# Second MoE layer: each expert's token rows formed by one-hot products on TensorE, in place of an indirect gather

## The reference, cut to what matters

```python
def _hier_moe(h, w_group, b_group, w_router, b_router, w_gate, w_up, w_down):
    ...
    p_in, e_in = lax.top_k(jax.nn.softmax(lg, axis=-1), TOP_K_IN_GROUP)
    ...
    xb = h_pad[tok_buf].reshape(n_blocks, MOE_BLOCK, d)

    def expert_block(args):
        xe, e = args
        return (jax.nn.silu(xe @ w_gate[e]) * (xe @ w_up[e])) @ w_down[e]

    y = lax.map(expert_block, (xb, blk_e)).reshape(cap, d)
    out = jax.ops.segment_sum(y.astype(jnp.float32) * w_buf[:, None], tok_buf, num_segments=t + 1)
```

## Time and profile before

| | us |
|---|---|
| median of 3 runs | 2418.37 (2416.91 to 2419.72) |
| profiled execution, own time | 2418.02 |
| its span | 2416.1 |
| PE busy, share of the span | 88% |
| DVE, ACT, POOL busy | 45%, 28%, 11% |
| mean DMA rate over the span | 273 GB/s |
| granted TensorE clock, mean over the span | 0.941 of full |

### The profile page before, as it was taken

The page is one execution under the profiler, slowest core; times in us unless marked ns, Lnnn a source line. Parts: engine busy times, 40 slices in busy tenths (PEclk is TensorE's granted clock), DMA queues, the critical chain, the costliest instruction groups (busy, mean ns, idle before and its releaser), DMA issues.

```text
span 2416.1 us, 29462 instructions
## 1 busy us (share of the span) xinstructions
PE 2128.9 (88%) x11370; PEld 1350.4 (56%) x11370; DVE 1089.0 (45%) x1709; ACT 676.7 (28%) x1071; POOL 256.0 (11%) x388
## 2 busy tenths in 40 slices
PE   7899999998899999989797878888789698888887
PEld 5777788886778888856532323333466333333332
DVE  6677754556676455586511111111686322211223
ACT  4243444343334433274211101110446100000000
POOL 2000000010000001000111111111120111111110
PEclk9989999999999999999698989999789699999998
DMA  9745566563656657402899999999911899999996
GB/s 312 261 162 197 196 222 201 202 247 124 239 175 226 209 182 255 107 1 76 309 368 401 414 408 410 403 410 374 296 24 55 346 381 412 423 413 415 416 409 244
DMA packets 178448, 659.87 MB, mean 273 GB/s; under 512 B 18375, under 2 KB 64023, under 8 KB 153136
## 3 DMA queue, kind: packets, MB, share of 16 engines
q1 hardware_dynamic: 159648, 622.65, 67.7%
q0 software_dynamic: 16592, 32.10, 4.2%
q10 hardware_dynamic: 2112, 3.77, 0.4%
HBM read 658.36 MB, written 24.84 MB: 283 GB/s over the span
## 4 chain that ended last, share of the span: by engine, by line
PE 53%; DMA 26%; DVE 12%; ACT 4%; issue 2%; SPq 1%; POOL 1%; ACTq 0%; POOLq 0%; DVEq 0%
PE bank L745 29%; DMA sb_ring<-in_w_up 23%; PE bank L1336 13%; DVE sb_ring_rounded L1978 2%; PE bank L759 2%; PE bank L1360 1%; PE bank L781 1%; ACT sb_hb L1572 1%; DVE sb_st L2182 1%; PE bank L1347 1%; DMA sb_ring<-in_ev_w_in 1%; PE bank L927 1%; PE bank L941 1%; DVE sb_ring_rounded L1985 1%; ACT sb_ring L1432 1%
## 5 line engine op out<-in xcount | busy, mean ns | idle before, releaser
L1336 PE MATMUL bank<-sb_ring,sb_arena 128*64 128x512 f32 x1984 | 508.3, 659 | 134.1 <-DMA sb_ring<-in_w_up 131.3
L745 PE MATMUL bank<-sb_ring_rounded,sb_hT_rounded 128*128 128x512 f32 x2432 | 605.4, 397 | 16.7 <-DVE sb_hT_rounded L1965 5.6
L745 PEld LDWEIGHTS bank<-sb_ring_rounded,sb_hT_rounded 128*128 128x128 f32 x2432 | 459.1, 191 | 116.7 <-issue 10.4
L1336 PEld LDWEIGHTS bank<-sb_ring,sb_arena 128*64 128x64 f32 x1984 | 155.8, 150 | 431.9 <-issue 424.4
L1978 DVE TENSOR_TENSOR sb_ring_rounded<-sb_ring,sb_ring_rounded 128x2048 fp32r<-128x2048 f32 (+1 forms) x142 | 314.9, 2258 | 109.6 <-ACT sb_ring_rounded L1467 105.0
L745 PE MATMUL bank<-sb_ring_rounded,sb_arena_rounded 128*128 128x512 f32 x1408 | 357.0, 395 | 7.7 <-DVE sb_arena_rounded L1965 7.2
L1467 ACT ACTIVATE sb_ring_rounded<-sb_ring 128x2048 fp32r<-128x2048 f32 x146 | 268.0, 1887 | 123.5 <-PE bank L745 98.9
L745 PEld LDWEIGHTS bank<-sb_ring_rounded,sb_arena_rounded 128*128 128x128 f32 x1408 | 266.1, 190 | 63.6 <-DVE sb_arena_rounded L1965 7.4
L1865 ACT ACTIVATE sb_hb<-bank 64x512 f32<-64x512 f32 x64 | 37.8, 590 | 758.6 <-PE bank L1336 758.6
L1360 PE MATMUL bank<-sb_ring,sb_arena 128*64 128x512 f32 x1008 | 230.1, 598 | 3.5 <-DVE sb_arena L2789 3.5
L2789 DVE COPY sb_arena<-bank 128x256 f32<-128x256 f32 x64 | 27.1, 424 | 374.2 <-PE bank L1347 374.2
(11 more groups left out here) (357 smaller groups left out, 1996.3 us busy)
## 6 DMA issues: line engine op xcount, KB each, us to landing
sb_ring<-in_w_down SPq DMA_DIRECT2D x63, 2048.0 KB, 23.1
sb_ring<-in_w_up SPq DMA_DIRECT2D x62, 2048.0 KB, 21.9
sb_ring<-in_w_gate SPq DMA_DIRECT2D x62, 2048.0 KB, 17.7
sb_ring<-in_w_ada SPq DMA_DIRECT2D x48, 1024.0 KB, 7.5
sb_ring<-in_ffn_w_gu SPq DMA_DIRECT2D x44, 1024.0 KB, 7.7
sb_ring<-in_xa_w_kv SPq DMA_DIRECT2D x16, 1024.0 KB, 7.3
sb_ring<-in_ffn_w_down SPq DMA_DIRECT2D x16, 1024.0 KB, 6.6
sb_ring<-in_od_w_in SPq DMA_DIRECT2D x12, 1024.0 KB, 7.5
```

Of the source, the lines that this page charges most:

```text
L745: ins = pe.matmul(bank[b][0:rows, :], rnd(x), rnd(w[:, k, :]), start=start and k == k0 and q == 0, stop=stop and k == k1 - 1 and q == len( ...
L1336: ins = pe.matmul(bank[2 * j + part][part * ROWS:(part + 1) * ROWS, :], mxT[:, j, k, :], w[:, k, :], start=k == 0, stop=k == KD - 1)
```

## The change

In layer 1 the rows of an expert no longer come from DRAM. VectorE turns each token's two pairs into a place number (`places`: 64 times its expert, plus its rank, plus 64 x 31 for every whole block of 64 that lies before it, minus a constant; four columns for two tiles and two picks), and `mark(j, e)` compares it with 64 constants: a 128 x 64 table per token tile that has a one where token p sits in row r of expert e. After every expert 64 is subtracted from all places. `place_rows` multiplies: for each of the 8 pieces of 128 features the two token tiles of `hr` are the stationary operand and the table is the moving one, and the sum of the two is the expert's rows, already turned. That is 16 products in place of 8 transposes. The table for e+2 is made in expert e's step on DVE; the products for e+1 stand where `turn_rows` stood. The first expert's table and products move ahead of the wait for `steps_ready`. Layer 1's store of the tokens to DRAM, the zeroing of `mx`, the gathers, and SP's wait for `rows0` go. `mact`, `mactT` and `mcol` get another home in layer 1, since the arena part that holds `hr` must stay. Layer 0 stays as it was.

```diff
             def experts(l):
                 m = moe[l]
-                pe.wait_ge(*c.next(s["steps_ready"]))
-                less_2 = steps_less_2(pe)
-                steps = less_2 + 2
-                for b in range(8):
-                    claim(b)
+                mact, mactT = act_home[l]
                 def turn_rows(j, e, landed_rows):
+                    if l == 1:
+                        place_rows(j, e)
+                        return
                     ...
+                def place_rows(j, e):
+                    pe.wait_ge(m["marked"], e + 1)
+                    pe.sem_inc(s["passed"], 1)
+                    for k in range(KD):
+                        for t in range(2):
+                            ins = pe.matmul(bank[T0 + j][:, k * ROWS:(k + 1) * ROWS], hr[:, t, k:D:KD], place_marks[:, j, t, :], start=t == 0, stop=t == 1)
+                    ins.then_inc(m["pe_xT"], 1)
+                if l == 1:
+                    claim(T0)
+                    place_rows(0, 0)
+                pe.wait_ge(*c.next(s["steps_ready"]))
...
@@ scalar
-                act.dma_start(DR["tok"][t * P:(t + 1) * P, :], hr[:, t, :]).then_inc(s[f"tok_stored{t % 2}"], 16)
+                if l == 0:
+                    act.dma_start(DR["tok"][t * P:(t + 1) * P, :], hr[:, t, :]).then_inc(s[f"tok_stored{t % 2}"], 16)
...
@@ vector
+            def mark(j, e):
+                m = moe[1]
+                if not (isinstance(e, int) and e == 0):
+                    dve.wait_ge(m["marked"], e)
+                    dve.tensor_scalar(places, places, -float(ROWS), None, ALU.add).then_inc(m["places"], 1)
+                    dve.wait_ge(m["places"], e)
+                since(dve, m["pe_xT"], e - 1)
+                row = cst[:, C_ROW:C_ROW + ROWS].unsqueeze(1).to_broadcast([P, 4, ROWS])
+                dve.tensor_tensor(place_equal, row, places.unsqueeze(2).to_broadcast([P, 4, ROWS]), ALU.is_equal).then_inc(m["equals"], 1)
+                dve.wait_ge(m["equals"], e + 1)
+                dve.tensor_tensor(place_marks[:, j, :, :], place_equal[:, 0:4:2, :], place_equal[:, 1:4:2, :], ALU.add).then_inc(m["marked"], 1)
...
@@ vector, route, after the blocks of each pair are counted
+                if l == 1:
+                    step(dve.tensor_scalar(places, mtmp[:, 3, 64:68], float(ROWS), -float(ROWS * N_EXP), ALU.mult, ALU.add))
+                    step(dve.tensor_tensor(places, places, rank, ALU.add))
+                    step(dve.scalar_tensor_tensor(places, whole_blocks, float(ROWS * (N_EXP - 1)), places, ALU.mult, ALU.add))
+                    mark(0, 0)
...
@@ vector, experts: once ahead of the loop, and at the end of expert e's step
+                if l == 1:
+                    mark(1, 1)
...
+                        if l == 1 and not last:
+                            mark(j, e + 2)
...
@@ gpsimd
-                    if not last:
+                    if l == 0 and not last:
                         gather(j, i * 2 + j + 2)
@@ sync
-                sp.wait_ge(m["rows0"], 16)
-                if l == 1:
+                if l == 0:
+                    sp.wait_ge(m["rows0"], 16)
+                else:
                     fetch(0, 2, 2)
```

More of the change, by code:

```diff
@@ L192, in loop_sems @@
         def loop_sems(l):
-            names = ["landed%d" % q for q in range(SLOTS + 2 + l)] + [
-                "rows0", "rows1", "stored0", "stored1", "pe_hidden", "pe_xT", "pe_aT", "pe_y_lo", "pe_y_hi",
-                "xT", "silu", "up", "acted", "aT", "y_lo", "y_hi", "my_free", "picked_in", "picked_out"]
+            by_rows = ["places", "equals", "marked"] if l else ["rows0", "rows1", "picked_in"]
+            names = ["landed%d" % q for q in range(SLOTS + 2 + l)] + by_rows + [
+                "stored0", "stored1", "pe_hidden", "pe_xT", "pe_aT", "pe_y_lo", "pe_y_hi",
+                "xT", "silu", "up", "acted", "aT", "y_lo", "y_hi", "my_free", "picked_out"]
             return {n: sem(f"moe{l}_{n}") for n in names}
@@ L453, in build_program @@
         mxT = view(2048, 2, KD, ROWS)
-        mact = view(4096, 2, EXP_H)
-        mactT = view(5120, 2, EXP_H // P, ROWS)
+        act_home = [(view(at, 2, EXP_H), view(at + 2 * EXP_H, 2, EXP_H // P, ROWS)) for at in (4096, 0)]
+        place_marks, place_equal = view(1536, 2, 2, ROWS), view(1792, 4, ROWS)
+        places = st[:, 72:76]
         mup = view(3072, 2, EXP_H)
@@ L467, in build_program @@
         BLK = CAP // ROWS
-        mcol = view(2 * D, 8, BLK, N_EXP)
+        mcols = [view(2 * D, 8, BLK, N_EXP), view(8192, 4, BLK, N_EXP)]
         mrow = view(11264, 8, ROWS)
@@ L1310, in route @@
                         pe.wait_ge(*c.next(s["marks_ready"]))
-                    ins = pe.matmul(bank[S1][0:ROWS, 0:BLK * N_EXP], rnd(mrow[:, q, :]), rnd(mcol[:, q, :, :]), start=q == 0, stop=q == 2 * tiles - 1)
+                    ins = pe.matmul(bank[S1][0:ROWS, 0:BLK * N_EXP], rnd(mrow[:, q, :]), rnd(mcols[l][:, q, :, :]), start=q == 0, stop=q == 2 * tiles - 1)
                 publish(ins, S1, "d")
@@ L1329, in turn_rows @@
                     ins.then_inc(m["pe_xT"], 1)
+                def place_rows(j, e):
[9 more added lines that the diff above has]
+                pe.wait_ge(*c.next(s["steps_ready"]))
+                less_2 = steps_less_2(pe)
+                steps = less_2 + 2
+                for b in range(8):
+                    if l == 0 or b != T0:
+                        claim(b)
                 def hidden(j, h, k0, k1):
@@ L1395, in own_products @@
                         ins.then_inc(s["own_full"], 1)
-                turn_rows(0, 0, 1)
+                if l == 0:
+                    turn_rows(0, 0, 1)
                 expert_steps(pe, less_2, pair)
@@ L1827, in route @@
                     turned(1)
-                zeros = cst[:, C_WIN0:C_WIN0 + P].unsqueeze(1).to_broadcast([P, 2 * KD, P])
-                act.activation(view(0, 2 * KD, P), zeros, ACT.Copy).then_inc(s["rows_zeroed"], 1)
+                if l == 0:
+                    zeros = cst[:, C_WIN0:C_WIN0 + P].unsqueeze(1).to_broadcast([P, 2 * KD, P])
+                    act.activation(view(0, 2 * KD, P), zeros, ACT.Copy).then_inc(s["rows_zeroed"], 1)
                 for t in range(0, tiles, tiles // 2):
@@ L1886, in experts @@
                     act.dma_start(DR["w"].rearrange("(t p j) -> p t j", p=P, j=2), mwt[:, 0:4].rearrange("p (t j) -> p t j", j=2)).then_inc(s["weights_stored"], 16)
-                turned_rows(0, 0)
+                if l == 0:
+                    turned_rows(0, 0)
                 expert_steps(act, less_2, pair)
@@ L2946, in experts @@
             tiles = 4 - 2 * l
-            for q in range(2):
-                pool.wait_ge(*c.next(s[f"tok_stored{q}"], 16 * tiles // 2))
+            if l == 0:
+                for q in range(2):
+                    pool.wait_ge(*c.next(s[f"tok_stored{q}"], 16 * tiles // 2))
             pool.wait_ge(*c.next(s["idx_ready"]))
@@ L3006, in pair @@
                         store(1 - j, i * 2 + j - 1)
-            gather(0, 0)
-            gather(1, 1)
+            if l == 0:
+                gather(0, 0)
+                gather(1, 1)
             pool.wait_ge(s["y_zeroed"], 64 * (l + 1))
@@ L3163, in _ @@
                     fill(0, I["g_final_2"])
-                pool.wait_ge(s["rows_zeroed"], l + 1)
+                if l == 0:
+                    pool.wait_ge(s["rows_zeroed"], 1)
                 experts(pool, c, step, l)
```

4 lines of the change are left out of this document (3 added, 1 removed).

## The result

The changed kernel takes 2586.88 us (median of 4 runs, 2581.95 to 2592.80) against 2417.68 us before (4 runs): 1.0693 times as long, 95% interval 1.0678 to 1.0709. It is 169 us slower. The prediction said 2415.7, with a range of 2410 to 2425.

A forecast was written before the change was run, and what follows sets the result against it. The prediction took PE as the bound early, then the DMA weight stream from expert 7. Restart +7.1, gathers -10.4 and lateness +0.6 make -2.7: 2418.02 to 2415.3, plus 0.35 to the median, 2415.7 us; range 2410 to 2425.

The forecast's parts named there:

- The slot of the 16 products: On PE, each later expert: products at 3.72 us replace transposes at 1.02, +2.70 us; PE's work 12.25 to 14.95.
- Rival A: Products cost more and PE becomes the bound; at 0.5 us more per slot, 2427 us; chance 0.18.
- I take the full clock: PE's products from expert 1 on run at clock 1.00; at half clock they would take about 7.0 us.
- Rival A's second step: In the expert loop PE becomes the bound: it sets the end above a 3.86 us slot, gain gone above 3.93.
- The start: hidden(0) begins 1.0 us earlier: 1.35 us of added DVE steps and 7.1 us of products replace the gather wait and transposes.
- Rival B: The clock rises during the first expert's products; hidden(0) ends 4.8 us earlier, total 2410.9 us; chance 0.10.
- The restart of the DMA: SP's issue of expert 5's gate, after hidden(3), moves from 1956.52 to 1963.6: +7.1 us.
- The gathers: In the DMA-bound stretch, 26 gathers removed at 0.40 us each: -10.4 us, period 15.69 to 15.29.
- rival C: The gathers were worth more, but PE caps the gain: 3.8 us before the forecast, 2411.9 us; chance 0.12.
- DVE's tables: Making the tables costs DVE some 1.1 us an expert, covered by its idle time; counted as nothing.
- the 35.3 us of the tail: After the last up matrix lands, 35.3 us remain to the end, which the change leaves alone.

The follow-up runs named there:

- experiment 1: The changed kernel with the stationary operand of the 16 products read as 128 contiguous columns, not every 8th (output differs): 2415.11 us.
- experiment 4: The kernel before, with the 8 transposes of an expert's rows reading contiguous columns instead of every 8th (output differs): 2418.87 us, one run.
- Experiment 2: The changed kernel, stride kept, with the moving operand of each product the same 64-column table four times over (256 columns; wrong rows): 2544.91 us.
- experiment 5: The kernel before with layer 1 gathers left out: those of experts 2 to 31, 2401.54 us; only odd experts from 3 on, 2408.78 us.
- stride2: The changed kernel with the stationary operand read as every 2nd of 256 columns, 8 bytes apart (output differs): 2423.57 us, one run.
- half_gather: The kernel before, without the layer 1 gathers of the odd experts from 3 on, those of the even ones kept (output differs): 2408.78 us.
- before_no_gather: The kernel before, without the gathers of experts 2 to 31 in layer 1 (output differs): 2401.54 us.
- contig: The same run as experiment 1: the changed kernel with the products' stationary operand read as contiguous columns, 2415.11 us.

## Why the prediction was wrong, point by point

**The slot of the 16 products: this failed.** "The nearest thing to the 16 products is an early stage with exactly their form", 3.72 us. Shape and type were the same, the reading of the stationary operand was not. It measured 7.80, and 7.51 for the first expert, where 7.1 was said. With the stride gone it is 3.71, to 0.01 what the earlier trace rows gave. This term is 130 us; with the 42 of the clock below it makes 171.8, from the 2415.11 of experiment 1 to the 2586.88 measured. Rival A named the stride but priced it at 0.5 us, from no row; the mechanism was at hand in the earlier trace rows, whose transposes load in 201 ns with it and 138 without (experiment 4).

**"I take the full clock": failed with it.** Rival A put the fall of the clock aside because "PE will be busy almost without a gap". PE was, and the clock fell all the same, inside every expert's products, and stayed low for the first 3 us of down. Experiment 2 prices it at 42 us. With contiguous columns and the same 64 moving columns the clock stays at 1.00, so this failure hangs on the first.

**Rival A's second step was right**: PE becomes the bound from a slot of 3.93 on, and it is, at 20.49 us an expert.

**The start: the parts were mis-sized slightly.** From the router's first weight load to the table products it was 1885.70 to 1900.84 in the earlier trace rows and 1880.77 to 1897.17 after: +1.26 us for 1.35. From the table products to hidden(0) it was 11.37 us and is now 9.68, so hidden(0) is 0.4 us earlier in all, where 1.0 was said. The rows after, and the same products in experiment 1:

```profile
1897.17 1.20 PE bank L1314 x4
1898.37 7.51 PE bank L1339 x32
1906.85 9.33 PE bank L1357 x32
1975.95 0.35 SPq L618 DMA_DIRECT2D sb_ring<-in_w_gate  x1
```
```profile
1905.07 6.74 PE bank L1339 x32
2374.42 3.43 PE bank L1357 x16
```

At half clock the stride adds 0.8 us to the 16 products (7.51 against 6.74), though the records of the loads hardly differ (335 ns against 333). Rival B, a clock that rises during the first products, did not come: it is 0.50 from 1898 to 1906. This profiled execution was 5.4 us ahead at hidden(0); the other 4.9 us arose before the router's products, which the change does not touch.

**The restart of the DMA: right in kind, mis-sized by the slot.** SP's issue for expert 5 came at 1975.95, 78.8 us behind the table products, against 55.7 before; with the 1.26 that is 24.4 us later, where 7.1 was said. With contiguous columns it is 60.2, so 5.8 later.

**The gathers: mis-sized, and capped.** 0.8 us each and not 0.40, 21 and not 10.4 us (experiment 5). The window of 3 us with one gather that I read can have caught only a part of its effect: that gather took 8.5 us from issue to landing. That a slow descriptor holds an engine's turn, the prediction's ground for 0.40, no run shows. The gain could not be had: in experiment 1 PE at 14.94 an expert and the stream at 14.91 are level, PE busy 360.00 of 360 us. That is rival C.

**"DVE's tables" and the 35.3 us of the tail.** The tables stayed hidden, PE has no wait for VectorE in the loop. The tail did not stay as it was; see below.

Experiment 1 came within 0.6 us of 2415.7, but not by my sum, and that is luck: hidden(31) started 3.7 us earlier than my 2378.1, and the part behind it was 3.2 us longer than my 35.3. By PE alone the prediction had hidden(31) start at 2374.3; it started at 2374.42. With the 3.8 us that rival C took off, 2411.9, and 3.4 more at the end, that makes 2415.3. PE's path set the end; the DMA's term was off by 10 us and didn't count.

## What to carry to other kernels

Price an instruction by a row whose operands are read in the same way, not only of the same shape: compare the subscripts behind both rows. On TensorE look at the weight loads apart from the products; where PEld is busy all of a stretch, its busy time over the number of loads is the price of one (here 240 ns with the stride and 117 without). The ns of a single record are not, since records overlap: 32 of 335 ns would make 10.7 us, and the slot is 7.80. Put the strided read on the operand, or in the layout, where it is read once, or turn the product round so that the small table is the stationary one; and before a wait for a transfer is taken away, work out how much PE work the bound leaves room for: once PE was the bound, the 0.2 us an expert of stride2 made 6 us.

## What the runs showed that I had not expected

- The record of a load of a 128 x 128 f32 stationary operand, in the median: 192, 196, 329, 335 ns at 4, 8, 16 and 32 bytes from column to column; the slot of the 16 products 3.71, 3.91, 7.66 and 7.80 us. At clock 0.50 the record is 333 ns at 4 bytes and 335 at 32.
- The granted clock fell from 1.00 to 0.50 in a stretch in which PE was busy throughout, 16 products of 64 columns with slow loads. It stayed at 1.00 with the same loads and 256 columns (experiment 2), and with 64 columns and fast loads (experiment 1).
- A gather of some 16 rows of 4 KB takes 0.8 us off a saturated weight stream, though its queue holds the engines for 0.22 an operation.
- From the start of the last VectorE step to the end of the span it is 7.0 us before (2409.08 to 2416.1), 5.8 in half_gather (2400.32 to 2406.1), 10.3 in before_no_gather (2389.82 to 2400.1), and 10.4 to 10.5 in every version with the products (2402.48 to 2412.9 in contig). The 5.8 fits none of the cases that were expected. The output's transfers land equally fast, 2.7 us, and no engine works in the difference. In before_no_gather it eats 3.3 us of what leaving the gathers out brings. What happens there stays open.
